# VectorE's steps in the first unit of each SwiGLU in another order

## The reference, cut to what matters

```python
def swiglu(x, wg, wu, wd):
    hid = jax.nn.silu(jnp.einsum('btd,df->btf', x, wg)) * jnp.einsum('btd,df->btf', x, wu)
    return jnp.einsum('btf,fd->btd', hid, wd)

x = layer_norm(ALPHA * x + 0.5 * swiglu(x, ffn1_wg, ffn1_wu, ffn1_wd), ln1_g, ln1_b)
...
x = layer_norm(ALPHA * x + jnp.einsum('btd,de->bte', m, w_out), ln2_g, ln2_b)
x = layer_norm(ALPHA * x + 0.5 * swiglu(x, ffn2_wg, ffn2_wu, ffn2_wd), ln3_g, ln3_b)
```

## Time and profile before

| | |
|---|---|
| median of 3 runs | 1044.84 us (1044.74 to 1045.28) |
| the profiled execution | 1046.54 us, span in the trace 1044.7 us |
| busy: TensorE, VectorE, ScalarE, GpSimd | 1031.5, 711.8, 482.5, 460.4 us |
| mean granted TensorE clock | 0.993 of full |
| chain that ended last | TensorE 93%, VectorE 3%, issue 1%, DMA 1% |
| loaded from HBM | 99.74 MB, 98 GB/s over the span |

### The profile page before, as it was taken

One profiled execution on the slowest core, in us unless ns is written; L12 is line 12 of the kernel. 1 busy time (PEld: TensorE's weight loads), 2 busy tenths in 40 slices (PEclk: granted clock), 3 DMA queues, 4 the chain that ended last, 5 costly groups with the idle time before them and its releaser, 6 DMA issues.

```text
span 1044.7 us, 21275 instructions
## 1 busy us (share of the span) xinstructions
PE 1031.5 (99%) x8592; PEld 1026.5 (98%) x8592; DVE 711.8 (68%) x1144; ACT 482.5 (46%) x735; POOL 460.4 (44%) x358
## 2 busy tenths in 40 slices
PE   8999999999999999999999999999999999999997
PEld 7999999999999999999999999999999999999997
DVE  6987977898755845822524325789888788977276
ACT  3665535645554452332332324456653565456335
POOL 4333444344348354844553546332425433443530
PEclk9999999999999999999999999999999999999999
DMA  8133343334327210532342334203333332432502
GB/s 256 52 102 102 102 121 87 103 97 122 112 83 195 82 40 13 156 103 85 87 117 67 113 89 127 67 14 102 91 112 102 102 116 77 132 101 82 144 20 82
DMA packets 195829, 103.32 MB, mean 99 GB/s; under 512 B 5188, under 2 KB 194260, under 8 KB 195725
## 3 DMA queue, kind: packets, MB, share of 16 engines
q1 hardware_dynamic: 195651, 101.86, 33.9%
q10 hardware_dynamic: 82, 0.12, 0.1%
HBM read 99.74 MB, written 2.48 MB: 98 GB/s over the span
## 4 chain that ended last, share of the span: by engine, by line
PE 93%; DVE 3%; issue 1%; DMA 1%; ACT 0%; SPq 0%; POOL 0%; DVEq 0%; ACTq 0%; POOLq 0%
PE ps L1641 19%; PE ps L1642 19%; PE ps L1643 19%; PE ps L1664 10%; PE ps L1661 10%; PE ps L1662 10%; PE ps L1710 2%; PE ps L1717 1%; PE ps L1711 1%; PE ps L1785 1%; DMA xrow<-in_x_prompt_dram 1%; PE ps L1764 1%; PE ps L2123 0%; DVE xl L1087 0%; DMA raw<-in_ffn_wg_dram 0%
## 5 line engine op out<-in xcount | busy, mean ns | idle before, releaser
L672 POOL TENSOR_TENSOR wl<-raw,wh 128x512 fp32r<-128x512 f32 (+1 forms) x168 | 223.9, 1362 | 328.7 <-DVE raw L1147 313.0
L719 ACT ACTIVATE wh<-raw 128x1024 fp32r<-128x1024 f32 (+4 forms) x183 | 210.4, 1154 | 175.0 <-DMA raw<-in_ffn_wg_dram 57.8
L1642 PE MATMUL ps<-form_lo,wh 128*128 128x260 f32 x640 | 181.5, 284 | 0.0
L1643 PE MATMUL ps<-form_hi,wl 128*128 128x260 f32 x640 | 181.3, 283 | 0.0
L1641 PE MATMUL ps<-form_hi,wh 128*128 128x260 f32 x640 | 181.3, 283 | 0.0
L1661 PE MATMUL ps<-xh,wh 128*128 128x260 f32 x640 | 166.9, 282 | 0.0
L1662 PE MATMUL ps<-xl,wh 128*128 128x260 f32 x640 | 166.5, 282 | 0.0
L1641 PE MATMUL ps<-xh,wh 128*128 128x260 f32 x536 | 152.1, 284 | 2.8 <-POOL wl L672 2.1
L1642 PE MATMUL ps<-xl,wh 128*128 128x260 f32 x536 | 151.8, 283 | 0.0
L1643 PE MATMUL ps<-xh,wl 128*128 128x260 f32 x536 | 151.5, 283 | 0.0
L659 POOL TENSOR_TENSOR wl<-raw,wh 128x512 fp32r<-128x512 f32 x63 | 88.0, 1396 | 138.9 <-ACT wh L719 138.8
(11 more groups left out here) (288 smaller groups left out, 2478.5 us busy)
## 6 DMA issues: line engine op xcount, KB each, us to landing
raw<-in_ffn_wg_dram SPq DMA_DIRECT2D x80, 256.0 KB, 3.3
raw<-in_w_in_dram SPq DMA_DIRECT2D x40, 512.0 KB, 4.0
b<-in_ffn_wu_dram SPq DMA_DIRECT2D x40, 256.0 KB, 3.4
raw<-in_ffn_wu_dram SPq DMA_DIRECT2D x40, 256.0 KB, 3.0
raw<-in_ffn_wd_dram SPq DMA_DIRECT2D x16, 512.0 KB, 5.5
raw<-in_ffn_wd_dram SPq DMA_DIRECT2D x24, 256.0 KB, 3.5
raw<-in_ffn_wd_dram SPq DMA_DIRECT2D x24, 192.0 KB, 2.9
raw<-in_w_out_dram SPq DMA_DIRECT2D x7, 512.0 KB, 3.8
```

The source lines that it names most:

```text
L672: nc.gpsimd.tensor_tensor(slots(wl_slot, s, p), slots(raw_slot, s, p), slots(wh_slot, s, p).bitcast(F32), ALU.subtract).then_inc(lo_ready, 1)
L719: return nc.scalar.activation(out, in_, ACT.Copy)
L1642: mm(out, hi, vl, start=False, stop=False, skip_group_check=more)
L1643: ins = mm(out, lo, vh, start=False, stop=n == count, skip_group_check=more)
```

## The change

`hid_opened(0)` and `hid_opened(1)` no longer stand ahead of the units but inside `first_unit()`, and the order there is another. The instructions, their operands and their waits are the same, on every engine. It applies to both SwiGLUs.

```diff
                 def first_unit():
                     t_two(n, 2)
+                    hid_opened(0)
+                    last_sum(n, 2)
+                    mid_sums(0, 1)
+                    hid_rest(0, 1)
+                    hid_opened(1)
                     rest_thirteen(n, 2)
-                    last_sum(n, 2)
-                    for f in range(2):
-                        mid_sums(f, (1, 3)[f])
-                        hid_rest(f, (1, 3)[f])
+                    mid_sums(1, 3)
+                    hid_rest(1, 3)
                     gate_first(1)
                     up_first(1)
                     rest_twenty_four(n, 2)
...
                 form_rest(n, 2)
                 form_rest(n, 3)
-                hid_opened(0)
-                hid_opened(1)
                 for p in range(1, NU + 1):
                     unit_steps(p)
```

## The result

The changed kernel took 1048.97 us in the median (1046.44 to 1056.04, 18 runs), the kernel before, beside it, 1044.87 us (1044.25 to 1049.01, 18 runs). The medians differ by 4.1 us. The ratio is 1.0036, with a 95% interval from 1.0021 to 1.005: slower, by 3.8 us (2.2 to 5.2). The forecast was 1048.7 us in a range from 1046.0 to 1049.7.

What follows compares the result with a forecast made beforehand. TensorE, busy 99% of the span, was taken as the bound. A gave +4.36 and B +3.43; their mean 3.9 on 1044.84 made 1048.7 us, range 1046.0 to 1049.7.

Steps and rivals of the forecast that it cites:

- Two deadlines: VectorE's steps in each SwiGLU: T4, through GpSimd, is needed for P1(2), and `up_second(1)` for Q4(1).
- Second SwiGLU, +1.57: Second SwiGLU: `up_second(1)` comes 1.57 us later, so Q4(1) starts at 720.44 instead of 718.87.
- The hole: Second SwiGLU: VectorE idles 2.0 us ahead of `mid_sums(0)`, waiting for ScalarE's `hid_up(0)`, with `rest_thirteen` queued behind.
- A: First SwiGLU: GpSimd's second rest goes before `rest_thirteen`; Q4(1) 0.21 us earlier, sum +4.36; taken by a little.
- B: First SwiGLU: VectorE's `rest_thirteen` goes before GpSimd's second rest; Q4(1) 1.14 us earlier, sum +3.43.
- 53.53 for full clock: First SwiGLU before the change: Q4(1) could start at 53.53 at full clock, against 54.05 measured.
- GpSimd and VectorE in each other's way: Both SwiGLUs: `rest_thirteen` beside GpSimd ends 1.08 us after GpSimd's running instruction; alone it takes 1.15.
- The clock: Half clock behind the gap ahead of Q4(1) in each SwiGLU, 1.5 us each, 3.0 in both; chance 0.55.
- the first rival: One clock drop, or drops partly inside a gap: 1.5 us less, +2.86 (A) or +1.93 (B); chance 0.3.
- +4.36: Whole kernel, sum in us for A with two clock drops: -0.21 + 1.57 + 2 x 1.5.
- The -0.21: First SwiGLU, A: Q4(1) starts 0.21 us earlier, at 53.84 instead of 54.05.
- A with 0.6 more: Top of the range, 1049.7 us: A with 0.6 for a further small wait behind a slower TensorE.

Runs made afterwards that it cites:

- experiment 4: `up_second(1)` moved ahead of `rest_twenty_four` of unit 2 in both SwiGLUs: ratio 1.0008 on the changed kernel, 0.9984 on the kernel before, both against the kernel before.
- after: The changed kernel of this study, against the kernel before: 1048.97 us, ratio 1.0036.
- before: The kernel without the change, measured beside the changed one: 1044.87 us.
- experiment 2: Changed kernel with `rest_thirteen` of unit 2 ahead of `mid_sums(0)` in both SwiGLUs: 1046.28 us, ratio 1.0002 to the kernel before.
- experiment 3: Changed kernel, GpSimd starting unit 2's rests only when `rest_thirteen` is done: 1048.25 us, ratio 1.0028 to the kernel before.
- look_before: A second profile of the kernel before, unchanged, taken for the clock: one execution, 1044.15 us.
- second_only: Kernel before with the changed order in the second SwiGLU only: 1047.54 us against 1046.1, ratio 1.0016.
- after_early_up: Changed kernel with `up_second(1)` ahead of `rest_twenty_four` of unit 2 in both SwiGLUs: 1046.9 us, ratio 1.0008 to the kernel before.
- up_after_rest: both_deadlines with the first SwiGLU's `up_second(1)` moved right behind `rest_thirteen` of unit 2: 1042.16 us, ratio 0.9968 to the kernel before.
- both_deadlines: Changed kernel, first SwiGLU's `hid_opened(1)` ahead of `mid_sums(0)`, second's old order, `up_second(1)` ahead of `rest_twenty_four` in both: 1043.01 us, ratio 0.9974 to the kernel before.
- both_again: both_deadlines measured once more, nothing changed, beside up_after_rest: ratio 0.9982 to the kernel before.
- pool_later: The run of experiment 3: changed kernel, GpSimd's unit 2 rests wait until `rest_thirteen` is done; 1048.25 us, ratio 1.0028 to the kernel before.
- after_again: The changed kernel measured once more beside the kernel before: 1048.7 us, ratio 1.0024.
- first_only: Kernel before with the changed order in the first SwiGLU only: 1046.4 us, ratio 1.0006.

## Why the prediction was right

- **Two deadlines** held. The gap ahead of P1(2) of the first SwiGLU went from 2.06 to 0.27 us, and the ones ahead of Q4(1) are 2.13 and 2.14 us. Moving `up_second(1)` alone (experiment 4) made Q4(1) 1.13 us earlier in the order of after, and 1.00 and 0.88 in that of before.
- **Second SwiGLU, +1.57**: measured +1.54. The hole was 1.92 (2.0 forecast). With `rest_thirteen` put into it (experiment 2), 0.97 of the 1.54 came back; without the overlap with GpSimd (experiment 3), VectorE's chain got only 0.23 shorter.
- **First SwiGLU, A or B**: A came. GpSimd's second rest began at 47.10 and `rest_thirteen` at 47.13, so it came second and took 2.35. P1(2) came 1.85 us earlier against VectorE, 1.86 forecast; Q4(1) 0.19 earlier, 0.21 forecast. That it is earlier at all is the drop in the profile of before, as the prediction's own 53.53 for full clock says. Without drops on either side the new order is later here, 9.55 against 9.22 in look_before and 9.24 in second_only, and 16.82 against 16.51 at P1(3).
- **GpSimd and VectorE in each other's way**: L1152 took 2.35 and 1.81, against 2.31 (47.62 to 49.93) and 1.84 (714.69 to 716.53) forecast. The Trainium skill ("SBUF — State Buffer", "SBUF: two separate sides") describes an exclusive lock between GpSimd and a VectorE instruction with two SBUF inputs. The profile after agrees with it: L1152 ended 1.08 us after GpSimd's second rest in the first SwiGLU and 1.09 after its last in the second. The overlap lengthened this step, but against before it cost little in sum, because what GpSimd did early it no longer did beside `rest_twenty_four` (2.12 and 2.03 before, 1.21 in both after).
- **The clock: the term that was mis-sized.** I took 1.5 us for each of two drops, 3.0 in sum, and gave that case 0.55. The price of one, 1.5, was right (1.54), but each of three profiles of the changed kernel has one drop in the first SwiGLU and none in the second. So the case of these profiles is the first rival, "one clock drop", at +2.86 with A. The measured differences of 3.8 (2.2 to 5.2) and 2.5 us (1.0 to 3.9) both hold it, and the second leaves out the +4.36 with two. The -0.21 counts on a drop in before, which only one of four profiles with that order has. An estimate from the profiles without and with drops: 0.31 + 1.54 for the order, 3/4 of 1.52 (16.82 to 18.34 at P1(3)) for the drops after, less 1/4 of 0.44 for those before, which is 2.9 us. That the point forecast of 3.9 came so near the first median is luck: it counts two drops where the profiles have one.
- **The page on the clock.** The page "TensorE: Matmul & The Clock Gate" of the Trainium skill, "HAM oscillation", has the clock fall only behind gaps longer than these. The drops behind 2.06 and 2.13 us contradict it; that the clock stayed full behind others of the same length doesn't make it right.
- **Sum.** From VectorE's first step to P2(2) the distance grew by 14.03 - 12.61 = 1.42 in the first SwiGLU and by 13.77 - 12.23 = 1.54 in the second, 3.0 us in sum. The spans differ by 1047.6 - 1044.7 = 2.9, but VectorE's first step also came 0.49 us earlier after (43.82 against 44.31), which the change doesn't touch, so 0.4 us of the difference behind it have no account here. The top of the range was meant to be A with 0.6 more, which is 1049.8, not 1049.7.

What stays open is why the first place has drops more often than the second. With so few profiles of each it may be chance.

## What to carry to other kernels

When a step is moved forward to end one wait, list every product that waits for the same engine further on, and compute when each of its last steps comes: moving work around ahead of a later deadline doesn't bring that deadline forward, but a wait moved forward puts it off, by as long as the engine idles. Put behind a wait whatever has the latest deadline, and ahead of it what fills the time; here that was one instruction of 0.4 us, `up_second(1)`, which 1.2 to 2 us of work with a later deadline stood before. Check the same order at each place where it is used: the two SwiGLUs ran the same code with different slack, and the order that cost 0.3 us in one (without clock drops) cost 1.5 us in the other. And measure a gain again a few products further on: of the 1.13 us that Q4(1) won in after_early_up 0.55 was left at unit 3, and of the 0.8 us of up_after_rest nothing.

## What was not expected of the hardware

The clock also falls in places that the change doesn't touch, and there it can outweigh the change. Two profiles of the same kernel, both_deadlines and both_again, have spans of 1040.6 and 1045.9 us. From VectorE's first step in the first SwiGLU to that in the second it is 661.92 us in the one and 666.60 in the other, 4.7 us more. Windows at the second LayerNorm, first both_deadlines:

```profile
662.00:667.30 5.30, 4.32 (x45) 4.11 (x44) 3.93 (x15) 2.53 (x5) 0.00 (x0) 1.00 0.01 3
667.30:677.60 10.30, 10.30 (x90) 10.30 (x89) 9.67 (x19) 5.97 (x12) 3.04 (x2) 1.00 0.35 103
```

and both_again:

```profile
662.00:667.30 5.30, 4.26 (x44) 4.06 (x43) 4.06 (x12) 2.57 (x6) 0.40 (x1) 1.00 0.01 5
667.30:677.60 10.30, 10.30 (x50) 10.30 (x50) 7.47 (x16) 4.40 (x9) 1.30 (x1) 0.50 0.16 46
```

TensorE had done about as much in the stretch before, and then ran for over 10 us at half clock in one execution, with 50 matmuls instead of 90, though it was busy throughout. Three of the fourteen profiles have that long stretch there (both_again, after_early_up, pool_later), four a stretch of 3.41 us at half clock (before, after, after_again, first_only), and seven none. How often it comes in the runs without a profile is not known. With differences of 1 to 4 us at stake, distances inside the profile told the experiments apart better than the medians did.
